# Gate and up projections as seven block products instead of eight, and the down projection in 16 jobs between them

## The reference

```python
def _swiglu(x, w_gu, w_down):
    a, b = jnp.split(x @ w_gu, 2, axis=-1)
    return (jax.nn.silu(a) * b) @ w_down

for i in range(DEPTH):                                  # DEPTH = 2
    x = x + 0.5 * _swiglu(_rmsnorm(x, norm_g[i, 0]), ffn_gu[i, 0], ffn_down[i, 0])
    m = retention(...) if i == 0 else gated_delta(...)  # of _rmsnorm(x, norm_g[i, 1])
    x = x + m
    x = x + 0.5 * _swiglu(_rmsnorm(x, norm_g[i, 2]), ffn_gu[i, 1], ffn_down[i, 1])
```

## Time and profile before

| | |
|---|---|
| median of 3 executions | 2615.48 us (2615.23 to 2615.69) |
| profiled execution, span from first to last instruction | 2619.2 us |
| PE, PE weight loads | busy 98% and 95% of the span |
| DVE | busy 48% |
| ACT | busy 31% |
| POOL | busy 11% |
| matmuls | 20575 |

### The profile page before, as it was taken

How to read it: one execution, slowest core, us unless ns; L and a number is a source line. 1 busy time by engine, 2 the same in 40 slices (tenths; PEclk the granted TensorE clock), 3 DMA queues, 4 the chain that set the end, 5 groups by cost and what they waited for, 6 DMA issues and landing times.

```text
span 2619.2 us, 48630 instructions
## 1 busy us (share of the span) xinstructions
PE 2572.6 (98%) x20575; PEld 2484.8 (95%) x20575; DVE 1264.2 (48%) x1584; ACT 821.0 (31%) x1042; POOL 300.5 (11%) x307
## 2 busy tenths in 40 slices
PE   8999999999999999999999999999999998999998
PEld 8999999898989899999999999989998998999998
DVE  5444334646464654443244443377557755444422
ACT  4222222424242432222232222244433344222222
POOL 1000010202020210000000000002530353000000
PEclk9999999999999999999999999999999999999999
DMA  4332334524242333332343323321122111323232
GB/s 131 96 96 76 88 93 141 185 86 177 93 173 97 137 91 87 96 86 78 97 111 91 96 82 89 104 84 52 49 66 87 36 49 53 97 84 93 78 91 74
DMA packets 340333, 246.73 MB, mean 94 GB/s; under 512 B 9428, under 2 KB 320908, under 8 KB 340208
## 3 DMA queue, kind: packets, MB, share of 16 engines
q1 hardware_dynamic: 325856, 197.32, 25.6%
q0 software_dynamic: 14352, 47.58, 5.0%
HBM read 218.81 MB, written 26.05 MB: 93 GB/s over the span
## 4 chain that ended last, share of the span: by engine, by line
PE 95%; DVE 3%; ACT 1%; issue 0%; DMA 0%; SPq 0%; ACTq 0%; DVEq 0%
PE ps L743 61%; PE ps L934 17%; PE ps L1118 5%; PE ps L828 1%; PE ps L851 1%; PE ps L837 1%; PE ps L1062 1%; PE ps L1128 1%; PE ps L783 1%; PE ps L1099 1%; DVE wl L1672 1%; PE ps L1075 1%; PE ps L993 0%; DVE xl L1678 0%; DVE cv L2012 0%
## 5 line engine op out<-in xcount | busy, mean ns | idle before, releaser
L743 PE MATMUL ps<-xh,wh 128*128 128x260 f32 x2816 | 569.0, 283 | 3.7 <-DVE gate L2258 1.5
L743 PE MATMUL ps<-xh,wl 128*128 128x260 f32 x2816 | 568.3, 284 | 0.0
L743 PE MATMUL ps<-xl,wh 128*128 128x260 f32 x2816 | 567.5, 283 | 0.0
L1672 DVE TENSOR_TENSOR wl<-raw,wh 128x2048 fp32r<-128x2048 f32 (+1 forms) x204 | 428.7, 2102 | 266.7 <-ACT wh L1333 266.5
L1333 ACT ACTIVATE wh<-raw 128x2048 fp32r<-128x2048 f32 (+1 forms) x204 | 354.5, 1738 | 343.2 <-PE ps L743 189.2
L743 PEld LDWEIGHTS ps<-xh,wh 128*128 128x128 f32 x2816 | 435.4, 189 | 5.8 <-issue 2.7
L743 PEld LDWEIGHTS ps<-xh,wl 128*128 128x128 f32 x2816 | 435.1, 189 | 0.0
L743 PEld LDWEIGHTS ps<-xl,wh 128*128 128x128 f32 x2816 | 433.8, 189 | 0.0
L743 PE MATMUL ps<-hh,wh 128*128 128x260 f32 x1408 | 284.4, 283 | 0.0
L743 PE MATMUL ps<-hh,wl 128*128 128x260 f32 x1408 | 283.1, 282 | 0.0
L743 PE MATMUL ps<-hl,wh 128*128 128x260 f32 x1408 | 282.8, 282 | 0.0
(11 more groups left out here) (372 smaller groups left out, 2857.8 us busy)
## 6 DMA issues: line engine op xcount, KB each, us to landing
raw<-in_ffn_gu_dram SPq DMA_DIRECT2D x176, 512.0 KB, 4.9
raw<-in_ffn_down_dram SPq DMA_DIRECT2D x64, 384.0 KB, 3.5
raw<-in_ret_w_in_dram SPq DMA_DIRECT2D x48, 512.0 KB, 4.4
raw<-in_ffn_down_dram SPq DMA_DIRECT2D x64, 320.0 KB, 3.9
s_ring<-in_state_ret_dram POOLq DMA_DIRECT2D x32, 512.0 KB, 6.2
out_dram<-s_ring POOLq DMA_DIRECT2D x32, 512.0 KB, 3.4
raw<-in_gdn_w_in_dram SPq DMA_DIRECT2D x32, 512.0 KB, 4.5
raw<-in_ret_w_out_dram SPq DMA_DIRECT2D x16, 512.0 KB, 3.8
```

Of the source, the lines that this page charges most:

```text
L743: m_ = nc.tensor.matmul(ps[:, 2 * q + h, 0:HALF], w_, v[:, kt0 + t, h * HALF:(h + 1) * HALF], start=b_, stop=e_)
L1672: nc.vector.tensor_tensor(wl[:, s, 0:cols], raw[:, s, 0:cols], wh[:, s, 0:cols].bitcast(F32), ALU.subtract).then_inc(w_low, 1)
```

## The change

The change replaces both FFN phases.

**Seven products.** Take for one tile pair the weights as a 2 x 2 block matrix (gate and up columns by even and odd tiles of x) and x as a 2 x 2 block matrix (even and odd tiles by the two halves of the tokens). Eight block products are replaced by seven (Winograd's form of Strassen's scheme), with sums of blocks as operands. A block product is 4 tiles x 3 matmuls of 260 columns, 12 matmuls; a gate/up job is 84 matmuls where it was 96. All sums are made before the split into high and low parts:

- of x, once for each FFN: ACT scales by the gains (`x_gained`, L1675), DVE makes four differences for each pair of tiles (`x_mixed`, L2123), ACT rounds and DVE subtracts seven blocks of 260 columns for each pair (`x_split`, L1680, L2131), into `xch` and `xcl`.
- of the weights, in every gate/up job: POOL makes four sums of 512 columns (`block_sum`, L744 to L754), into `mixed` or in place in `raw`. ACT and DVE then split seven blocks of 512 columns (`block_split`, L1695, L2136) in five instructions, groups A, 1, 2, 4, L, where before it was one of 2048 columns.
- of the results: some products are added in PSUM onto others. ACT copies three partial results of 260 columns out (`copy`, L1729) before the next product is added onto their bank, and DVE adds them (L2181, L2186, L2191). Then come scaling of one result (L2196), silu on ACT in PSUM (L1733), scaling again (L2200), two products of 260 columns (L2205, L2210), `hh` (L1743) and `hl` (L2215).

**Jobs.** The down projection is still computed with eight block products. It is cut into 16 jobs: 4 groups of contraction tiles x 4 pairs of output tiles, of 48 matmuls (first group) or 72 (the others), 24 for each pair of `hh` tiles. `hh` and `hl` keep only 12 tiles. Each FFN runs the jobs in one order, written G (gate/up) and D (down): G x5, D G D G D G D, G x3, D G D G D G, G x2, D, D x4. Gate/up product 4 of a job runs after the first product of the next job.

**Loops.** The four FFNs are written out on all engines without loops. Memory is laid out again; the mixers keep their instructions. Their first `wh`/`wl` split moves to the last job of the FFN before.

The core of the diff:

```diff
+def ffn_jobs():
+    G = lambda a_, b_: [("G", q, (0, 1, 2, 3)) for q in range(a_, b_)]
+    D_ = lambda m, pairs_: [("D", m, pairs_)]
+    out = G(0, 5)
+    for q, pairs_, more in ((5, (0, 1), 3), (11, (2, 3, 4), 3)):
+        for m in range(4):
+            out += D_(m, pairs_) + G(q + m, q + m + 1) if m < 3 else D_(m, pairs_)
+        out += G(q + 3, q + 3 + more)
...
+def gate_order(j):
+    return (1, 5, 2, 6, 3, 7) if j == 0 else (1, 2, 6, 5, 7, 3)
...
+            def block_sum(f, j, n):
...
+                if n == "1":
...
+                    m_ = tt(s_, a21, a22, ALU.add)
+                if n == "3":
+                    m_ = tt(a21, a11, a21, ALU.subtract)
+                if n == "2":
+                    pool.wait_ge(blk_low, blocks_split(f, j, "A"))
...
+                    m_ = tt(a11, s_, a11, ALU.subtract)
+                if n == "4":
+                    pool.wait_ge(blk_low, blocks_split(f, j, "1"))
...
+                    m_ = tt(s_, a12, a11, ALU.subtract)
...
+                def product(c, m, steps=range(KP)):
...
+                        if m in (1, 2, 5):
+                            bank_free(c, m)
+                        elif m == 4:
+                            v(f"C22.{c}")
+                        else:
+                            act_({6: "m1", 7: "u2", 3: "m5"}[m] + f".{c}")
+                        pe.wait_ge(blk_low, blocks_split(f, c, PRODUCT_GROUP[m]))
...
+                    for t in steps:
...
+                        for n, (w_, r_) in enumerate(((hi_w, high), (hi_w, low), (lo_w, high))):
+                            m_ = nc.tensor.matmul(o, w_, r_, start=m in (1, 2, 5) and t == 0 and n == 0,
+                                                  stop=t == KP - 1 and n == 2, skip_group_check=m in (3, 4, 6, 7))
...
+                for j in range(1, NJ):
+                    if not is_gate(j):
+                        down(j)
+                        continue
+                    for m in gate_order(j):
+                        product(j, m)
+                        if m == 1 and is_gate(j - 1):
+                            product(j - 1, 4)
...
-                            for g, t_ in ((0, gate), (1, up)):
-                                dve.wait_ge(parts_done, ph.unit_done(ph.unit0 + 2 * j + g))
-                                nc.vector.tensor_tensor(halves(t_[:]), pair(g), halves(rinv[:]), ALU.mult).then_inc(acc_free, 1)
```

More of the change, by code:

```diff
@@ new lines, with down_blocks, blocks_of, uses_of @@
+SPLITS_BEFORE = [sum(len(groups_of(c)) for c in range(j)) for j in range(NJ + 1)]
+def down_blocks(j):
+    return (3, 5, 4) if is_gate(j - 1) or not down_blocks(j - 1)[0] else (0, 1, 2)
+def blocks_of(j, group):
+    if not is_gate(j):
+        return (down_blocks(j)["xyz".index(group)],)
+    return GROUP_BLOCKS.get(group, (5, 6 + JOBS[j][1] % 2))
+def uses_of(j):
+    if not is_gate(j):
+        return {down_blocks(j)[i]: f"P{i}.{j}" for i in range(len(JOBS[j][2]))}
+    uses = {b: f"{m}.{j}" for m, b in PRODUCT_BLOCK.items()}
+    uses[6 + JOBS[j][1] % 2] = f"4.{j}"
+    return uses
@@ new lines, in last_use, with ffn_t_names @@
+def last_use(f, j, b):
+    for c in range(j - 1, -1, -1):
+        if b in uses_of(c):
+            return uses_of(c)[b], f
+    for c in range(NJ - 1, -1, -1):
+        if f == 2 and b in uses_of(c):
+            return uses_of(c)[b], f - 1
+    return None
+def gate_order(j):
+    return (1, 5, 2, 6, 3, 7) if j == 0 else (1, 2, 6, 5, 7, 3)
+def ffn_t_names():
+    out = []
+    for j in range(NJ):
+        before = [f"4.{j - 1}"] if is_gate(j - 1) else []
+        if is_gate(j):
+            first, *rest = (f"{m}.{j}" for m in gate_order(j))
+            out += [first] + before + rest
+        else:
+            last = len(JOBS[j][2]) - 1
+            out += before + [f"P{i}.{j}" for i in range(last)] + [f"X.{j}", f"P{last}.{j}"]
+    return " ".join(out)
@@ new lines, in ffn_v_names @@
+def ffn_v_names():
+    out = []
+    for j in range(NJ + 1):
+        p, gate_before = j - 1, is_gate(j - 1)
+        if is_gate(j):
+            if j and not gate_before:
+                out += [f"XA.{p}", f"XB.{p}"]
+            if gate_before:
+                out += [f"sr.{p}", f"hB.{p}", f"hA.{p}"]
+            out.append(f"C11.{j}")
+            if gate_before:
+                out.append(f"hl.{p}")
+            out += [f"C12.{j}", f"C22.{j}", f"gr.{j}"] if j == 0 else [f"C22.{j}", f"C12.{j}", f"gr.{j}"]
+        elif gate_before:
+            out += [f"sr.{p}", f"hB.{p}", f"hA.{p}", f"hl.{p}"]
+        else:
+            out += [f"XA.{p}", f"XB.{p}"]
+    return " ".join(out)
@@ L85, with ffn_a_names @@
+def ffn_a_names():
+    out = []
+    for j in range(NJ):
+        before = is_gate(j - 1)
+        if before:
+            out.append(f"silu.{j - 1}")
+        if is_gate(j):
+            out.append(f"m1.{j}")
+        if before:
+            out.append(f"hh.{j - 1}")
+        if is_gate(j):
+            out += [f"m5.{j}", f"u2.{j}"] if j == 0 else [f"u2.{j}", f"m5.{j}"]
+    return " ".join(out)
+FFN_T = Steps(ffn_t_names())
+FFN_V = Steps(ffn_v_names())
+FFN_A = Steps(ffn_a_names())
 GH, GG, GC, LV = 8, 4, 4, 6
@@ L525, in _ @@
+            ffn(0)
+            ret_body(phases[0], 0)
+            with sp.Fori(1, RH) as h:
+                ret_body(phases[0], h)
+            ffn(1)
+            ffn(2)
+            for g in range(2):
+                gdn_body(phases[1], g)
+            ffn(3)
             for c, (done, n) in enumerate(((y_by_v, 1), (y_by_a, 1), (y_by_v, 2), (y_by_v, 3))):
@@ L1659, in _ @@
+            ffn(0)
+            ret_body(phases[0], 0, False)
+            with act.Fori(1, RH - 1) as h:
+                ret_body(phases[0], h, False)
+            ret_body(phases[0], RH - 1, True)
+            ffn(1)
+            ffn(2)
+            root_of(phases[1].norm - 1)
+            for g in range(2):
+                gdn_body(phases[1], g, g == 1)
+            ffn(3)
+            y_copied(KT - 1)
             act.wait_ge(ssq_sum, 7)
[L1660 removed]
@@ L2285, in _ @@
+            ffn(0)
+            ret_body(phases[0], 0, False)
+            with dve.Fori(1, RH - 1) as h:
+                ret_body(phases[0], h, False)
+            ret_body(phases[0], RH - 1, True)
+            ffn(1)
+            ffn(2)
+            gdn_pre(phases[1])
+            for g in range(2):
+                gdn_body(phases[1], g, g == 1)
+            ffn(3)
             dve.wait_ge(y_roots, 2)
```

1043 lines of the change are left out of this document (679 added, 364 removed).

## The result

| | before | after |
|---|---|---|
| median of the runs | 2615.59 us | 2685.97 us (2682.56 to 2693.75) |
| ratio | | 1.0273 [1.0256, 1.0289] |
| span of the profiled execution | 2619.2 us | 2692.2 us |

The account below looks back on a forecast made before the run. PE was taken to bound the FFNs, at 0.1202 us a matmul. The sum was 2619.2 - 126.9 + 36 + 30 = 2558.3 us profiled, 3.7 less for the runs' median: 2554.6 us, range 2503 to 2600.

Parts of the forecast that it names:

- What goes: Gate/up jobs have 84 matmuls instead of 96; 1056 matmuls fewer at 0.1202 us each, 126.9 us saved.
- A pair of D and G is safe: In D-G pairs PE has 15.9 us of work and DVE 13.5, so no PE wait was expected.
- POOL's sums: In gate/up jobs, four sums delay DVE's two-input instructions by 4 x 1.05 x 0.65 us, taking DVE to 11.0 us.
- Granted clock: PE was taken to stay at 2.4 GHz, every FFN matmul costing 0.1202 us; no term for a lower clock.
- Rival 4: PE does not keep 0.1202: more weight changes add 0.002 us per gate/up matmul, giving 2570 us; chance 0.02.
- Runs of G: Consecutive gate/up jobs take 11.1 us, 1.0 over PE, at 9 jobs in each of four FFNs: +36 us.
- The starts: At each FFN's start, DVE's x work and job 1's reciprocal delay PE: +30 us together, between +10 and +45.
- rival 3: Slower than before: ACT's queued copies delay all 88 gate/up jobs; at 1.5 us a job, 2651 us; chance 0.05.
- rival 2: DVE and POOL in turn: sums delay DVE by 1.05 us each, jobs between D jobs wait 0.2; 2590 us; chance 0.13.
- The three cases that shared it: Forecast 2554.6 us (0.58); POOL's sums falling where DVE waits anyway, 2506 (0.22); DVE and POOL in turn, 2590 (0.13).

Follow-up runs that it names:

- e5: Changed kernel with POOL's four weight sums cut to 8 columns and DVE's two down-job additions ahead of splits 2 and L; 2549.0 us, 0.9740 of before.
- e2: Changed kernel with DVE's two down-job additions ahead of the next gate/up job's splits 2 and L; 2634.6 us, 1.0093 of the kernel before.
- e1: Changed kernel with POOL's four weight sums cut from 512 to 8 columns, groups 1 and 4 split from loaded weights; 2612.5 us, 0.9986 of before.
- e3: Changed kernel with the four weight sums made by DVE instead of POOL, just ahead of the splits needing them; 2699.6 us, 1.0335 of before.
- e7: Changed kernel with ACT's copies of products 1 and 5 of job 0 ahead of x's last rounding and group L; 2686.0 us, 1.0263 of before.
- e8: Changed kernel with down-job additions first on DVE, job 0's first copies early and product 7's copy ahead of group A on ACT; 2647.2 us.

## Why the prediction was wrong

- **What goes: right.** 1056 matmuls fewer, and the FFNs' sum closes to 0.2 us with 126.9 for them. With the sums left out and the additions moved up, e5, the FFNs are 68.3 us faster than before (1569.1 - 1500.8), where the forecast was 126.9 - 36 - 30 = 60.9. That these are near each other is chance, since the forecast had 36 us in it for the sums, which e5 leaves out.
- **"A pair of D and G is safe": the step that failed.** It compared sums, 15.9 us of PE with 13.5 of DVE, and the sums did not fail: in one such pair, from 1053.3 to 1071.7 us, DVE is busy for 11.5. But product 2 needs the addition of the down job after 12 of the gate/up job's 84 matmuls, and what stood ahead of it in DVE's queue was never listed, as had been done for product 7. The 16 waits are 44 us, where the prediction had none. The matmuls at half clock right behind them, counted in the change's rows, add 21, so the step cost about 65, and e2 gave 55 back by order alone. At the fourths POOL's sums have a part too, 1.1 to 1.5 us each (e1).
- **Granted clock: not in the sum at all.** I had kept 0.1202 for all matmuls. 590 in the FFNs took about 0.22: +59.6 us, nearly as much as the two terms that I did estimate together, 36 and 30. Rival 4 was about PE's speed, with the wrong reason.
- **POOL's sums: the mechanism right, the price low.** Sums of 1.3 us take up to 1.8 in the mean where DVE works, and DVE waits as foreseen:

```profile
L746 POOL TENSOR_TENSOR raw<-raw 128x512 f32<-128x512 f32 x88 | 160.6, 1825 | 0.0
L744 POOL TENSOR_TENSOR mixed<-raw 128x512 f32<-128x512 f32 x88 | 129.9, 1476 | 481.0 <-DMA raw<-in_ffn_gu_dram 462.0 <-DVE yl L2434 18.9
```

  L744 and L746 are the sums 1 and 3, of 512 columns. Leaving them out gives 72.9 us of FFN time (e1), half clock and waits at the starts with them, where I had 36 for the runs and part of 30 for the starts. The delay of DVE itself was not priced low: DVE is busy for 153.0 us more than in e1, 1.7 for each of the 88 jobs if all is put on them, where I had 4 x 1.05 x 0.65 = 2.7. It was its effect on PE, through waits at the starts and the clock behind them, that I had too low. Moving the sums into DVE's own queue is no better (e3).
- **Runs of G: somewhat too dear.** I had 36 waits of 1.0 us and in job 1 of each FFN 1.7 + 1.9. Seen: 1.8, 1.6 and 1.7 in jobs 1 to 3, then one wait of 1.0 to 1.1 in each run, 33 us together against 48. That place and price, the copies for product 7, were read rightly.
- **The starts: too cheap, the second term that was mis-sized.** I had job 0 end 33.9 us after the first write of x in the first FFN (42.6 us), 33.9 after it behind the retention layer and 31.8 behind gdn. Measured to the end of product 7 it is 46.4 us (at 55.65), 45.4 and 43.1, so each of these three starts is 11 to 13 us dearer than forecast. The largest part is the 16 differences of 260 columns. They had 7.2 us in the sum and take 15.1 behind the retention layer, and 12.2 in e1, where POOL makes no full sums. The rows of these instructions alone, first the change, then e1 (window, us, DVE's busy us and instructions, clock, share and GB/s of the DMAs):

```profile
938.00:983.60 45.60, 15.09 (x16) 0.81 0.17 47
```

```profile
924.80:965.90 41.10, 12.24 (x16) 0.88 0.18 52
```

  I had added up DVE's work evenly; in the rows PE stops twice in job 0, for `xcl` and then for `kept`, 8.1, 8.6 and 9.3 us in all at these starts, and 10.1 at the third FFN, mostly for `x`. In the first FFN there are 9.7 us more before the first products.
- **Which rival.** The side was rival 3's (0.05), and its point of 1.1 us a job beyond 30 us for the starts was passed ((130.2 + 59.6 - 30) / 88 = 1.8). Its mechanism, ACT's copies in every job, was not: with copies made first, e7's median did not move, and e8 was slower than e2. A wait of D-G pairs was in rival 2, at 0.2 us instead of 2.4.

I gave 0.92 to faster. The three cases that shared it differed in the size of one term, and none in a term left out.

## What to carry to other kernels

When work moves off a full engine, list for each thing that engine will wait for what stands ahead of it in the other engine's queue, and who releases that; a comparison of busy sums shows only that a queue can keep up, not that it is in time. Price a new wait of PE like those of 2.4 us here at about one and a half times its length (44 us of waits, 21 of half clock behind them). And when one part of a program is edited, cut the trace so that the parts that are not edited can be compared by themselves.
